# Expert stage of a hybrid decoder step: eight row slots, each waited for on its own, and groups of four experts

## The chip, the cores and the metric

The kernel runs on one core of a Trainium2 chip. The time is the device time of one launch in microseconds (us). Before the change it was 5759.28 us, the median of three runs (5758.3 to 5764.06).

## What is computed

One layer of a decoder: modulated norm, one wide projection, two token mixers, a merge with an output projection, and then an expert layer. Prompt: 1024 tokens of width 1024. Sample group: 8 tokens. The change touches the expert layer alone. For each token it has 8 heads, for each head 16 expert numbers `e` and 16 gates `g` (found earlier), out of 16384 experts. An expert is a row `u` and a row `v` of 1024 float32 numbers each.

```
def one_block(args):
    hb, eb, gb = args
    a = jax.nn.gelu(jnp.einsum('td,thkd->thk', hb, u[eb], preferred_element_type=jnp.float32))
    return jnp.einsum('thk,thkd->td', (gb * a).astype(v.dtype), v[eb])
...
y = rms_norm(x + g2 * peer_ffn(h2, ...), final_g)
```

## The kernel before

The program is a row of stages with a barrier between them: modulation and projection, the prompt's mixers, the sample's mixers, merge and routing, and then `experts`, which starts at about 3025 us and runs to the end. In DRAM the `u` and `v` of an expert stand side by side in one row of 8 KB (`peer_uv`).

The prompt is 8 tiles of 128 tokens, one token on each partition. A tile has 8 heads (`PH`), a head 16 experts (`TOPK`, here `NSLOT`). I call the gather of one expert number for the 128 tokens of a tile a *row load*: one indirect DMA on the GpSimd queue (POOL), 128 rows of 8 KB, 1 MB, into one of the slots `UV[n]` (128 partitions x 2048 numbers). There are 8 x 8 x 16 = 1024 row loads. Each goes through the same steps:

- POOL (L1542 to L1547) waits until the slot is free, which TensorE's semaphore `vdone` tells, and issues the load. Slot `n` holds expert `n` of the head; the waits stand at every fourth expert (`GRP`), and each wants four slots free.
- DVE (L1671 to L1687) waits for a group of four loads (`loaded[n // GRP]`), and multiplies each `u` half with the token's row `h2` and sums it, a *dot* (L1677). After every eighth dot (`SUB`) it works out the weights of those eight: three small steps of the gelu (L1447 to L1449), a tanh on ScalarE (ACT, L1612), two more small steps (L1684, L1687).
- ACT makes from each weight column a diagonal matrix 128 x 128 (L1617).
- TensorE (PE, L1586 to L1592) multiplies the diagonal with the `v` half into a PSUM accumulator, 2 products of 512 columns for each expert, which stand in the trace as four records. Behind the last of them it raises `vdone`, and the slot is free.

The accumulators are `ex_acc` for even tiles, `ex_bc` for odd ones. After the first head of a tile the DVE and ACT programs do the end of the tile before it (`tail`): gate, residual, final norm, store. The order of each engine is written out by hand; nothing is scheduled by a planner.

Ahead of the prompt the stage works the sample's 8 tokens: 8 loads (L1534) into slots 8 to 15 (`HALF + n`), dots, and products (L1572). While it does so, `vdone` already allows the prompt's first eight loads into slots 0 to 7 (`HALF`, L1557); the other eight come free when the sample's last product is done (L1576, L1577).

Of the kernel before, what the change touches and what calls it, by code (L numbers as in the profile page):

```python
# [14 lines left out]
P = 128  # L15
D = 1024
# [3 lines left out]
NS = 8  # L20
# [12 lines left out]
PH, NK, DQ, TOPK = 8, 128, 128, 16  # L33
# [17 lines left out]
def at_least(eng, sem, value):  # L51

    if not isinstance(value, int) or value > 0:
        eng.wait_ge(sem, value)
# [1397 lines left out]
def experts(k, misc):  # L1452

    nc = k.nc
    NSLOT = TOPK
    GRP = 4
    NQ = NSLOT // GRP
    HALF = NSLOT - NS
    names = ("in", "mod", "idxT_ps", "idxT", "bc", "bc_used", "dots", "s_u", "s_exp", "steps", "wm", "s_sum", "s_t", "x1", "sq", "var", "root", "y", "h2_l", "x1_l",
             "staged", "dotted", "g_steps", "g_u", "g_exp", "w", "diag", "vdone", "zero", "tail_t", "t_steps", "y_out", "h2s", "nsel", "tiles_done")  # L1460
    s = {n: k.sem("ex_" + n) for n in names}
    rows_s = [k.sem(f"ex_rows_sample{n}") for n in range(NS)]
    loaded = [k.sem(f"ex_rows_loaded{q}") for q in range(NQ)]
    uv_dram = k.i["peer_uv"]
    SUB = NSLOT // 2
    with k.phase() as f:
        UV = [f.sb(f"ex_UV{n}", [P, 2 * D]) for n in range(NSLOT)]
# [6 lines left out]
        idx = [f.sb(f"ex_idx{b}", [P, NSLOT], U32) for b in range(2)]  # L1474
# [21 lines left out]
        with nc.Block() as block:  # L1496
# [32 lines left out]
            @block.gpsimd  # L1529
            def _(pool):  # L1530

                pool.wait_ge(s["idxT"], 1)
                for n in range(NS):
                    pool.indirect_dma_start(out=UV[HALF + n][:, :], out_offset=None, in_=uv_dram, in_offset=bass.IndirectOffsetOnAxis(ap=idxT[:, n:n + 1], axis=0)).then_inc(rows_s[n], 16)  # L1534


                def head(i, pair, b):

                    h = pair * 2 + b
                    nc.gpsimd.tensor_copy(idx[b][:, :], k.idx[:, bass.ds(i * P + h * NSLOT, NSLOT)]).then_inc(p["staged"], 1)  # L1540
                    pool.wait_ge(p["staged"], i * PH + h + 1)
                    for n in range(NSLOT):  # L1542
                        if n % GRP == 0:
                            pool.wait_ge(p["vdone"], (i * PH + h) * NSLOT + n + GRP)
                            pool.sem_inc(p["zero"], 1)
                        pool.indirect_dma_start(out=UV[n][:, :], out_offset=None, in_=uv_dram,  # L1546
                                                in_offset=bass.IndirectOffsetOnAxis(ap=idx[b][:, n:n + 1], axis=0)).then_inc(loaded[n // GRP], 16)  # L1547

                with pool.Fori(0, TILES) as i:
                    with pool.Fori(0, PH // 2) as pair:  # L1550
                        for b in range(2):
                            head(i, pair, b)

            @block.tensor
            def _(pe):

                pe.sem_inc(p["vdone"], HALF)  # L1557
                nc.tensor.transpose(tp[:, 0:NS], k.idx_s[:, :], ident[SL, SL])
                nc.tensor.transpose(tp[:, NS:2 * NS], k.gate_s[:, :], ident[SL, SL]).then_inc(s["idxT_ps"], 1)
                pe.wait_ge(s["h2s"], 16)  # L1560
                pe.wait_ge(s["nsel"], 1)
                for n in range(NS):
                    at_least(pe, s["dots"], n - 1)
                    for b in range(2):
# [12 lines left out]
                pe.sem_inc(p["vdone"], NSLOT - HALF)  # L1577
                pe.wait_ge(s["tiles_done"], 2)

                def tile(i, j, t):  # L1580
                    acc = accs[t]
                    pe.wait_ge(p["acc_t"], i if not isinstance(i, int) else 1)
                    for b in range(2):
                        nc.tensor.matmul(acc[:, b, :], zb[:, :], zr[:, :], start=True, stop=False)
                    with pe.Fori(0, PH) as h:
                        for n in range(NSLOT):  # L1586
                            if n % GRP == 0:
                                pe.wait_ge(loaded[n // GRP], (i * PH + h) * (16 * GRP) + 16 * GRP)
                            pe.wait_ge(p["diag"], (i * PH + h) * NSLOT + n + 1)
                            for b in range(2):  # L1590
                                last = nc.tensor.matmul(acc[:, b, :], dg[:, n, :], V[n][:, b * 512:(b + 1) * 512], start=False, stop=False)  # L1591
                            last.then_inc(p["vdone"], 1)  # L1592
                    for b in range(2):
                        last = nc.tensor.matmul(acc[:, b, :], zb[:, :], zr[:, :], start=False, stop=True)
                    last.then_inc(p["summed"], 1)
                pairs_of_tiles(pe, tile)

            @block.scalar
            def _(act):
# [7 lines left out]


                def head(i, h):
                    for c in range(2):  # L1610
                        act.wait_ge(p["g_u"], (i * PH + h) * 2 + c + 1)
                        nc.scalar.activation(uu[:, c * SUB:(c + 1) * SUB], uu[:, c * SUB:(c + 1) * SUB], ACT.Tanh, scale=GELU_C).then_inc(p["g_exp"], 1)  # L1612
                        act.wait_ge(p["w"], (i * PH + h) * 2 + c + 1)
                        for n in range(c * SUB, (c + 1) * SUB):

                            act.wait_ge(p["vdone"], (i * PH + h) * NSLOT + n + 1)
                            nc.scalar.activation(dg[:, n, :], ident, ACT.Copy, scale=w[:, n:n + 1]).then_inc(p["diag"], 1)  # L1617

                def tail(i):
# [18 lines left out]
            def _(dve):  # L1638
# [3 lines left out]
                link = chained(dve, s["steps"])  # L1642
# [26 lines left out]
                dve.sem_inc(p["acc_t"], 1)  # L1669

                def head(i, h, hb):  # L1671
                    for c in range(2):
# [8 lines left out]
                        link = chained(dve, p["g_steps"], (i * PH + h) * 6 + c * 3)  # L1681
                        gelu_steps(nc, link, a[:, cols], t[:, cols], uu[:, cols]).then_inc(p["g_u"], 1)
                        dve.wait_ge(p["g_exp"], (i * PH + h) * 2 + c + 1)
                        link(nc.vector.scalar_tensor_tensor(out=t[:, cols], in0=uu[:, cols], scalar=1.0, in1=a[:, cols], op0=ALU.add, op1=ALU.mult))  # L1684
                        gate = k.gate[:, bass.ds(i * P + h * NSLOT + c * SUB, SUB)]
                        at_least(dve, p["diag"], (i * PH + h) * NSLOT + c * SUB - SUB)
# [90 lines left out]
```

## Time and profile before

| | us |
|---|---|
| median of the runs | 5759.28 |
| the profiled execution, its own time | 5768.66 |
| span of its trace | 5766.5 |
| busy in the span: PE | 4560.9 (79%) |
| busy: DVE | 2323.8 (40%) |
| busy: POOL | 1169.3 (20%) |
| busy: ACT | 886.2 (15%) |
| row loads, 1024, POOL | 1083.11 MB on queue q0 |

The profiled execution took 9.4 us longer than the median. Busy shares of the whole span mix stages of quite different kinds, so the stage of the experts is read by itself: first its DMA share and the rate of its transfers, then the times at which single groups land and single slots come free.

### The profile page before, as it was taken

The page shows a single profiled execution, that of the slowest core. Times are in us where ns is not written, and L with a number is a line of the kernel's source. Part 1 is how long each engine was busy: PE and PEld are TensorE (multiplying, and loading weights), DVE is VectorE, ACT ScalarE, POOL GpSimd, SP SyncE. Part 2 cuts the span into 40 slices and gives each one's busy share as a digit, 9 for nine tenths or more (in the row PEclk, how much of TensorE's full clock was granted, in tenths as well). Part 3 has the DMA queues.
Part 4 walks back from the last instruction along what each step waited for, and adds up shares of the span by engine and source line. Part 5 has one row for each costly group of instructions (what it writes and reads, how often), then busy time and mean ns, then how long its engine had stood idle before and what let it go on. Part 6 is the DMA issues. An engine that isn't in the chain of part 4 may idle for free. (4 is left out here: it accounts for less than half of the span.)

```text
span 5766.5 us, 41916 instructions
## 1 busy us (share of the span) xinstructions
PE 4560.9 (79%) x13011; PEld 2177.4 (38%) x13044; DVE 2323.8 (40%) x5481; ACT 886.2 (15%) x1951; POOL 1169.3 (20%) x1104
## 2 busy tenths in 40 slices
PE   6999999977777767888837777777777777777777
PEld 1444444434544543344312333333333333333333
DVE  2000000003333334388894554454544445454544
ACT  1100000012222220121101111111111111111111
POOL 0000000000000000000004444444444444444443
PEclk8999999987777776899977888888888898889888
DMA  7143444462101023311009999999999999999997
GB/s 260 53 156 136 149 156 156 166 208 92 42 35 57 31 76 136 140 47 47 28 3 367 411 409 412 405 402 400 407 401 401 407 408 412 408 411 410 410 405 313
DMA packets 247745, 1409.28 MB, mean 244 GB/s; under 512 B 24467, under 2 KB 76179, under 8 KB 110804
## 3 DMA queue, kind: packets, MB, share of 16 engines
q0 software_dynamic: 148896, 1083.11, 46.0%
q1 hardware_dynamic: 72118, 272.53, 13.4%
q10 hardware_dynamic: 26672, 52.88, 2.4%
q8 instruction: 33, 0.54, 0.0%
q14 instruction: 26, 0.21, 0.0%
HBM read 1341.66 MB, written 159.08 MB: 260 GB/s over the span
## 5 line engine op out<-in xcount | busy, mean ns | idle before, releaser
L1677 DVE CUSTOM_DVE_ANT_0 ex_UV<-ex_UV,ex_h 128x1024 f32<-128x1024 f32 x1024 | 1194.0, 1221 | 1211.9 <-DMA ex_UV<-in_peer_uv,ex_idx 1211.9
L1546 POOL DMA_INDIRECT ex_UV<-in_peer_uv,ex_idx x1024 | 1135.0, 1108 | 1534.5 <-PE ex_acc L1591 630.5
L1591 PE MATMUL ex_acc<-ex_UV,ex_diag 128*128 128x512 f32 x2048 | 1015.8, 659 | 320.2 <-ACT ex_diag L1617 320.2
L1591 PE MATMUL ex_bc<-ex_UV,ex_diag 128*128 128x512 f32 x2048 | 1008.9, 656 | 318.1 <-ACT ex_diag L1617 318.1
L406 PE MATMUL z_ps<-win,hT 128*128 128x464 f32 x2688 | 1055.2, 554 | 22.3 <-ACT z_stage L383 11.6
L1591 PEld LDWEIGHTS ex_acc<-ex_UV,ex_diag 128*128 128x128 f32 x2048 | 429.3, 213 | 905.8 <-issue 526.6
L1591 PEld LDWEIGHTS ex_bc<-ex_UV,ex_diag 128*128 128x128 f32 x2048 | 425.9, 211 | 899.7 <-issue 519.6
L406 PEld LDWEIGHTS z_ps<-win,hT 128*128 128x128 f32 x2688 | 510.9, 191 | 555.9 <-issue 537.4
L763 DVE TENSOR_SCALAR mx_gn<-mx_gn 128x1024 f32<-128x1024 f32 x1 | 0.7, 694 | 1136.8 <-DMA mx_gn<-in_gla_gn_g 1136.8
L1534 POOL DMA_INDIRECT ex_UV<-in_peer_uv,ex_idxT x8 | 7.6, 953 | 1740.9 <-DVE ex_idxT L1646 1738.8
L1612 ACT ACTIVATE ex_u<-ex_u 128x8 f32<-128x8 f32 x128 | 26.7, 209 | 2130.0 <-DVE ex_u L1449 2130.0
L1617 ACT ACTIVATE ex_diag<-misc,ex_w 128x128 f32<-128x128 f32 x1024 | 312.9, 388 | 88.8 <-DVE ex_w L1687 88.8
L488 POOL DMA_DIRECT2D mx_masks<-table_masks x1 | 0.7, 706 | 1274.8 <-POOLq L150 1274.8
L383 ACT COPY z_stage<-z_ps 128x464 f32<-128x464 f32 x168 | 91.6, 546 | 991.5 <-PE z_ps L406 961.5
L1218 PE MATMUL rt_G<-rt_wO,rt_Tg 128*128 128x512 f32 (+1 forms) x288 | 146.7, 674 | 9.2 <-ACT rt_Tg L1270 9.2
L819 DVE TENSOR_REDUCE mx_max<-mx_big 128x1 f32<-128x1920 f32 x32 | 69.0, 2158 | 162.4 <-PE mx_big L622 162.4
L1218 PE MATMUL rt_G<-rt_wQ,rt_Tg 128*128 128x512 f32 (+1 forms) x288 | 127.2, 600 | 9.1 <-ACT rt_Tg L1270 9.1
L1218 PE MATMUL rt_G<-rt_wA,rt_Tm 128*128 128x512 f32 (+1 forms) x288 | 128.1, 604 | 7.8 <-DMA rt_wA<-in_w_branch_a 7.8
L636 PE MATMUL mx_T<-misc,mx_P 128*128 128x128 f32 x480 | 68.0, 285 | 66.3 <-DVE mx_PT L832 55.9
L615 PE MATMUL mx_big<-mx_kT,mx_qT 128*128 128x512 f32 x128 | 88.8, 784 | 28.0 <-DVE mx_kT L761 26.4
L1218 PEld LDWEIGHTS rt_G<-rt_wO,rt_Tg 128*128 128x128 f32 (+1 forms) x288 | 58.2, 206 | 92.5 <-issue 81.0
L653 PE MATMUL mx_O<-mx_V,mx_PT 128*128 128x128 f32 (+1 forms) x480 | 79.9, 343 | 11.2 <-DVE mx_PT L832 6.7
(332 smaller groups left out, 3399.5 us busy)
## 6 DMA issues: line engine op xcount, KB each, us to landing
out_kv_w_sample<-in_cache_kv_w SPq DMA_DIRECT2D x8, 8188.0 KB, 42.7
win<-in_w_in SPq DMA_DIRECT2D x21, 1856.0 KB, 11.4
z_scratch<-z_stage ACTq DMA_DIRECT2D x21, 1856.0 KB
ada<-in_ada_w SPq DMA_DIRECT2D x12, 2048.0 KB, 7.8
ex_UV<-in_peer_uv,ex_idx POOLq DMA_INDIRECT x1024, 8.5
out_kv_w_sample<-in_cache_kv_w SPq DMA_DIRECT2D x8, 2044.0 KB, 18.1
mx_zg<-z_scratch SPq DMA_DIRECT2D x8, 1544.0 KB, 7.1
mx_zq<-z_scratch SPq DMA_DIRECT2D x8, 1536.0 KB, 10.1
```

The source lines that it names most:

```text
L383: nc.scalar.copy(zst[u][:, t, :], pz[t % NBK][:, 0:W]).then_inc(evac, 1)
L406: last = nc.tensor.matmul(pz[t % NBK][:, 0:W], hT[:, c, t * P:t * P + P], w[u][:, c, :], start=(c == 0), stop=(c == KD - 1))
L615: nc.tensor.matmul(big[:, b, :], qT[:, 8 + h, :], kT[:, 8 + h, b * 512:(b + 1) * 512], start=False, stop=True)
L636: last = nc.tensor.transpose(Tb[b % 2][:, (j % 4) * P:(j % 4 + 1) * P], Pm[:, j * P:(j + 1) * P], ident)
L653: last = nc.tensor.matmul(OM[h % 2][:, 0:HD], PT[h % 2][:, j, :], vv, start=(j == 0), stop=(j == KT - 1))
L819: nc.vector.reduce_max(mx[:, h:h + 1], sc_all[:, 0:NKEY], AX.X).then_inc(s["max_steps"], 1)
L1218: last = nc.tensor.matmul(G[0:R, bank + b, :], T[:, off + c, 0:R], w[:, c, b * 512:(b + 1) * 512], start=(c == 0), stop=(c == n - 1))
L1546: pool.indirect_dma_start(out=UV[n][:, :], out_offset=None, in_=uv_dram, in_offset=bass.IndirectOffsetOnAxis(ap=idx[b][:, n:n + 1], axis=0 ...
L1591: last = nc.tensor.matmul(acc[:, b, :], dg[:, n, :], V[n][:, b * 512:(b + 1) * 512], start=False, stop=False)
L1612: nc.scalar.activation(uu[:, c * SUB:(c + 1) * SUB], uu[:, c * SUB:(c + 1) * SUB], ACT.Tanh, scale=GELU_C).then_inc(p["g_exp"], 1)
L1617: nc.scalar.activation(dg[:, n, :], ident, ACT.Copy, scale=w[:, n:n + 1]).then_inc(p["diag"], 1)
L1677: nc.vector.tensor_tensor_reduce(out=U[n], in0=U[n], in1=hb, scale=1.0, scalar=0.0, op0=ALU.mult, op1=ALU.add, accum_out=a[:, n:n + 1]).th ...
```

## The change

There are eight slots in place of sixteen. Expert `n` of a head goes into slot `n % 8`. Each slot has a semaphore of its own, and DVE, PE and POOL wait for each single slot where they waited for four. The weights of a head are worked out in four groups of four experts (`SUB = 4`) where there were two of eight. The sample's 8 loads now take all eight slots (`HALF = 8 - 8 = 0`), so that the line that allowed eight of the prompt's loads ahead of the sample's end falls away.

```
-    GRP = 4
-    NQ = NSLOT // GRP
-    HALF = NSLOT - NS
+    NBUF = 8
+    ROUNDS = NSLOT // NBUF
+    HALF = NBUF - NS
...
-    SUB = NSLOT // 2
+    SUB = 4
+    SUBS = NSLOT // SUB
...
                     for n in range(NSLOT):
-                        if n % GRP == 0:
-                            pool.wait_ge(p["vdone"], (i * PH + h) * NSLOT + n + GRP)
-                            pool.sem_inc(p["zero"], 1)
-                        pool.indirect_dma_start(out=UV[n][:, :], out_offset=None, in_=uv_dram,
-                                                in_offset=bass.IndirectOffsetOnAxis(ap=idx[b][:, n:n + 1], axis=0)).then_inc(loaded[n // GRP], 16)
+                        pool.wait_ge(p["vdone"], (i * PH + h) * NSLOT + n + 1)
+                        pool.sem_inc(p["zero"], 1)
+                        pool.indirect_dma_start(out=UV[n % NBUF][:, :], out_offset=None, in_=uv_dram,
+                                                in_offset=bass.IndirectOffsetOnAxis(ap=idx[b][:, n:n + 1], axis=0)).then_inc(loaded[n % NBUF], 16)
...
-                pe.sem_inc(p["vdone"], HALF)
...
                 pe.wait_ge(s["s_sum"], 1)
-                pe.sem_inc(p["vdone"], NSLOT - HALF)
+                pe.sem_inc(p["vdone"], NBUF - HALF)
...
-                            if n % GRP == 0:
-                                pe.wait_ge(loaded[n // GRP], (i * PH + h) * (16 * GRP) + 16 * GRP)
+                            pe.wait_ge(loaded[n % NBUF], ((i * PH + h) * ROUNDS + n // NBUF) * 16 + 16)
...
-                    for c in range(2):
+                    for c in range(SUBS):
...
-                            act.wait_ge(p["vdone"], (i * PH + h) * NSLOT + n + 1)
+                            at_least(act, p["vdone"], (i * PH + h) * NSLOT + n + 1 - (NSLOT - NBUF))
...
-                            if n % GRP == 0:
-                                dve.wait_ge(loaded[n // GRP], (i * PH + h) * (16 * GRP) + 16 * GRP)
-                            nc.vector.tensor_tensor_reduce(out=U[n], in0=U[n], in1=hb, scale=1.0, scalar=0.0, op0=ALU.mult, op1=ALU.add,
+                            dve.wait_ge(loaded[n % NBUF], ((i * PH + h) * ROUNDS + n // NBUF) * 16 + 16)
+                            nc.vector.tensor_tensor_reduce(out=U[n % NBUF], in0=U[n % NBUF], in1=hb, scale=1.0, scalar=0.0, op0=ALU.mult, op1=ALU.add,
```

How this stands on the engines, at the two places that matter. First POOL, the first loads of a prompt head, before (`ex_UV4` is slot 4, `ep_vdone` the semaphore of the free slots):

```order
L1546 DMA ex_UV0<-in_peer_uv,ex_idx0 128x2048 [waits ep_vdone]
L1546 DMA ex_UV1<-in_peer_uv,ex_idx0 128x2048
L1546 DMA ex_UV2<-in_peer_uv,ex_idx0 128x2048
L1546 DMA ex_UV3<-in_peer_uv,ex_idx0 128x2048
L1544 REGISTER_ALU
L1546 DMA ex_UV4<-in_peer_uv,ex_idx0 128x2048 [waits ep_vdone]
```

And in the changed kernel:

```order
L1546 DMA ex_UV0<-in_peer_uv,ex_idx0 128x2048 [waits ep_vdone]
L1544 REGISTER_ALU
L1546 DMA ex_UV1<-in_peer_uv,ex_idx0 128x2048 [waits ep_vdone]
L1544 REGISTER_ALU
L1546 DMA ex_UV2<-in_peer_uv,ex_idx0 128x2048 [waits ep_vdone]
L1544 REGISTER_ALU
L1546 DMA ex_UV3<-in_peer_uv,ex_idx0 128x2048 [waits ep_vdone]
```

A load can now be issued as soon as its one slot is free, where it waited for the fourth of its group; the ninth load of a head goes into slot 0 again, where it had slot 8.

Second DVE, in a tile's first head, around the first weights. Before (each dot is an `ISA` row with a second one that reads the sum; semaphores have kept the names of an earlier stage, `mx_T_free0` is here the one of loads 8 to 11):

```order
L1677 ISA ex_UV6,ex_a<-ex_UV6,ex_h20 128x1024
L1677 ISA ex_a 128x1
L1677 ISA ex_UV7,ex_a<-ex_UV7,ex_h20 128x1024
L1677 ISA ex_a 128x1
L1447 TENSOR_TENSOR ex_t<-ex_a 128x8 [waits sm_state_loaded3]
L1448 TENSOR_SCALAR ex_t<-ex_t 128x8 [waits sm_state_loaded4]
L1449 TENSOR_TENSOR ex_u<-ex_t,ex_a 128x8 [waits sm_state_loaded4]
L1684 SCALAR_TENSOR_TENSOR ex_t<-ex_u,ex_a 128x8 [waits sm_state_loaded6]
L1687 SCALAR_TENSOR_TENSOR ex_w<-ex_t,expert_gate 128x8 [waits sm_state_loaded4]
L1677 ISA ex_UV8,ex_a<-ex_UV8,ex_h20 128x1024 [waits mx_T_free0]
```

And in the changed kernel (`mx_T_free1` is the semaphore of slot 3, `sm_state_loaded1` that of slot 4):

```order
L1674 ISA ex_UV3,ex_a<-ex_UV3,ex_h20 128x1024 [waits mx_T_free1]
L1674 ISA ex_a 128x1
L1447 TENSOR_TENSOR ex_t<-ex_a 128x4 [waits sm_state_loaded7]
L1448 TENSOR_SCALAR ex_t<-ex_t 128x4 [waits ep_g_steps]
L1449 TENSOR_TENSOR ex_u<-ex_t,ex_a 128x4 [waits ep_g_steps]
L1681 SCALAR_TENSOR_TENSOR ex_t<-ex_u,ex_a 128x4 [waits ep_g_exp]
L1684 SCALAR_TENSOR_TENSOR ex_w<-ex_t,expert_gate 128x4 [waits ep_g_steps]
L1674 ISA ex_UV4,ex_a<-ex_UV4,ex_h20 128x1024 [waits sm_state_loaded1]
```

The weights follow the fourth dot, where they followed the eighth, and every dot has a wait of its own.

## Rows read from the trace of the kernel before

**Rows 1.** Windows: busy time by engine, two stretches of the prompt's experts.
```profile
core 0: us, PE busy (x) PEld busy (x) DVE busy (x) ACT busy (x) POOL busy (x), PEclk, DMA share, GB/s
3440.00:4440.00 1000.00, 763.06 (x1528) 322.07 (x1530) 500.12 (x1022) 162.14 (x465) 423.81 (x404) 0.87 0.99 405
4440.00:5440.00 1000.00, 757.34 (x1555) 320.28 (x1558) 501.05 (x1025) 162.19 (x465) 431.96 (x410) 0.88 1.00 409
```

**Rows 2.** Timeline of DVE in one head: start, length, first dots of groups.
```profile
4165.11 1.23 DVE L1677 CUSTOM_DVE_ANT_0 ex_UV<-ex_UV,ex_h 128x1024 f32<-128x1024 f32 x1 [6.11 <-DMA ex_UV<-in_peer_uv,ex_idx]
...
4175.05 1.22 DVE L1677 CUSTOM_DVE_ANT_0 ex_UV<-ex_UV,ex_h 128x1024 f32<-128x1024 f32 x1 [5.27 <-DMA ex_UV<-in_peer_uv,ex_idx]
...
4178.49 1.22 DVE L1677 CUSTOM_DVE_ANT_0 ex_UV<-ex_UV,ex_h 128x1024 f32<-128x1024 f32 x1
...
4184.99 1.22 DVE L1677 CUSTOM_DVE_ANT_0 ex_UV<-ex_UV,ex_h 128x1024 f32<-128x1024 f32 x1 [3.63 <-DMA ex_UV<-in_peer_uv,ex_idx]
```

**Rows 3.** Timeline of POOL in the same head: issues of row loads.
```profile
4150.99 0.96 POOL L1546 DMA_INDIRECT ex_UV<-in_peer_uv,ex_idx  x1 [12.34 <-PE ex_bc L1591]
...
4155.17 1.99 POOL L1546 DMA_INDIRECT ex_UV<-in_peer_uv,ex_idx  x1 [0.30 <-issue]
...
4192.35 0.96 POOL L1546 DMA_INDIRECT ex_UV<-in_peer_uv,ex_idx  x1 [10.28 <-PE ex_bc L1591]
```

**Rows 4.** Windows of 5 us in the same head, columns as in rows 1.
```profile
4140.00:4145.00 5.00, 4.84 (x6) 2.19 (x7) 2.10 (x3) 2.15 (x8) 0.00 (x0) 0.50 1.01 423
...
4150.00:4155.00 5.00, 5.00 (x13) 2.28 (x12) 2.17 (x3) 0.00 (x0) 3.27 (x3) 1.00 0.58 195
```

**Rows 5.** The line of the row loads, L1546: summary, and issue to landing.
```profile
L1546 POOL DMA_INDIRECT ex_UV<-in_peer_uv,ex_idx x1016: 932/938/10366, 3080.0 to 5719.1; - x170
...
DMA to landing us min/median/max: 5.4/8.4/12.1
```

**Rows 6.** Timeline of PE: three bursts of eight experts, 32 records each.
```profile
4140.16 16.87 PE L1591 MATMUL ex_bc<-ex_UV,ex_diag 128*128 128x512 f32 x32 [9.29 <-ACT ex_diag L1617]
4159.57 15.70 PE L1591 MATMUL ex_bc<-ex_UV,ex_diag 128*128 128x512 f32 x32 [2.54 <-ACT ex_diag L1617]
4181.93 16.47 PE L1591 MATMUL ex_bc<-ex_UV,ex_diag 128*128 128x512 f32 x32 [6.66 <-ACT ex_diag L1617]
```

**Rows 7.** Chain that ended last: start, length; PE for four experts, then POOL.
```profile
3115.61 7.15 PE ex_acc L1591 x16
...
4159.57 8.84 PE ex_bc L1591 x16
...
4169.21 1.37 POOL ex_UV L1546
```

**Rows 8.** DMA issues: KB each, us to landing.
```profile
ex_h<-h_scratch SPq DMA_DIRECT2D x8, 512.0 KB, 12.4
ex_x<-x_scratch SPq DMA_DIRECT2D x8, 512.0 KB, 8.2
out_y_prompt<-ex_y ACTq DMA_DIRECT2D x8, 512.0 KB, 9.2
```

**Rows 9.** Timeline of POOL at the start of the prompt's experts.
```profile
3046.16 0.93 POOL L1546 DMA_INDIRECT ex_UV<-in_peer_uv,ex_idx  x1 [0.30 <-issue]
3079.96 0.94 POOL L1546 DMA_INDIRECT ex_UV<-in_peer_uv,ex_idx  x1 [32.86 <-PEq L1577]
```

**Rows 10.** Timeline of DVE at a tile's end: last dot, last weights, first dot behind the tail.
```profile
3774.39 1.22 DVE L1677 CUSTOM_DVE_ANT_0 ex_UV<-ex_UV,ex_h 128x1024 f32<-128x1024 f32 x1
...
3776.94 0.17 DVE L1687 SCALAR_TENSOR_TENSOR ex_w<-ex_t,expert_gate 128x8 f32<-128x8 f32 x1
...
3783.65 1.22 DVE L1677 CUSTOM_DVE_ANT_0 ex_UV<-ex_UV,ex_h 128x1024 f32<-128x1024 f32 x1
```

**Rows 11.** Timeline of DVE at the end of the kernel.
```profile
5755.40 1.23 DVE L1696 TENSOR_TENSOR ex_y<-ex_bc,ex_g 128x1024 f32<-128x1024 f32 x1 [16.73 <-PE ex_bc L1594]
```

More of the change, by code:

```diff
@@ L1462, in experts @@
     rows_s = [k.sem(f"ex_rows_sample{n}") for n in range(NS)]
-    loaded = [k.sem(f"ex_rows_loaded{q}") for q in range(NQ)]
+    loaded = [k.sem(f"ex_slot_loaded{n}") for n in range(NBUF)]
     uv_dram = k.i["peer_uv"]
-    SUB = NSLOT // 2
+    SUB = 4
+    SUBS = NSLOT // SUB
     with k.phase() as f:
-        UV = [f.sb(f"ex_UV{n}", [P, 2 * D]) for n in range(NSLOT)]
+        UV = [f.sb(f"ex_UV{n}", [P, 2 * D]) for n in range(NBUF)]
         U = [t[:, 0:D] for t in UV]
@@ L1586, in tile @@
                         for n in range(NSLOT):
-                            if n % GRP == 0:
-                                pe.wait_ge(loaded[n // GRP], (i * PH + h) * (16 * GRP) + 16 * GRP)
+                            pe.wait_ge(loaded[n % NBUF], ((i * PH + h) * ROUNDS + n // NBUF) * 16 + 16)
                             pe.wait_ge(p["diag"], (i * PH + h) * NSLOT + n + 1)
                             for b in range(2):
-                                last = nc.tensor.matmul(acc[:, b, :], dg[:, n, :], V[n][:, b * 512:(b + 1) * 512], start=False, stop=False)
+                                last = nc.tensor.matmul(acc[:, b, :], dg[:, n, :], V[n % NBUF][:, b * 512:(b + 1) * 512], start=False, stop=False)
                             last.then_inc(p["vdone"], 1)
@@ L1609, in head @@
                 def head(i, h):
-                    for c in range(2):
-                        act.wait_ge(p["g_u"], (i * PH + h) * 2 + c + 1)
+                    for c in range(SUBS):
+                        act.wait_ge(p["g_u"], (i * PH + h) * SUBS + c + 1)
                         nc.scalar.activation(uu[:, c * SUB:(c + 1) * SUB], uu[:, c * SUB:(c + 1) * SUB], ACT.Tanh, scale=GELU_C).then_inc(p["g_exp"], 1)
-                        act.wait_ge(p["w"], (i * PH + h) * 2 + c + 1)
+                        act.wait_ge(p["w"], (i * PH + h) * SUBS + c + 1)
                         for n in range(c * SUB, (c + 1) * SUB):
-                            act.wait_ge(p["vdone"], (i * PH + h) * NSLOT + n + 1)
+                            at_least(act, p["vdone"], (i * PH + h) * NSLOT + n + 1 - (NSLOT - NBUF))
                             nc.scalar.activation(dg[:, n, :], ident, ACT.Copy, scale=w[:, n:n + 1]).then_inc(p["diag"], 1)
@@ L1671, in head @@
                 def head(i, h, hb):
-                    for c in range(2):
+                    for c in range(SUBS):
                         cols = slice(c * SUB, (c + 1) * SUB)
                         for n in range(c * SUB, (c + 1) * SUB):
-                            if n % GRP == 0:
-                                dve.wait_ge(loaded[n // GRP], (i * PH + h) * (16 * GRP) + 16 * GRP)
-                            nc.vector.tensor_tensor_reduce(out=U[n], in0=U[n], in1=hb, scale=1.0, scalar=0.0, op0=ALU.mult, op1=ALU.add,
+                            dve.wait_ge(loaded[n % NBUF], ((i * PH + h) * ROUNDS + n // NBUF) * 16 + 16)
+                            nc.vector.tensor_tensor_reduce(out=U[n % NBUF], in0=U[n % NBUF], in1=hb, scale=1.0, scalar=0.0, op0=ALU.mult, op1=ALU.add,
                                                            accum_out=a[:, n:n + 1]).then_inc(p["dotted"], 1)
@@ L1680, in head @@
                         dve.sem_inc(p["dots_done"], SUB)
-                        link = chained(dve, p["g_steps"], (i * PH + h) * 6 + c * 3)
+                        link = chained(dve, p["g_steps"], ((i * PH + h) * SUBS + c) * 3)
                         gelu_steps(nc, link, a[:, cols], t[:, cols], uu[:, cols]).then_inc(p["g_u"], 1)
-                        dve.wait_ge(p["g_exp"], (i * PH + h) * 2 + c + 1)
+                        dve.wait_ge(p["g_exp"], (i * PH + h) * SUBS + c + 1)
                         link(nc.vector.scalar_tensor_tensor(out=t[:, cols], in0=uu[:, cols], scalar=1.0, in1=a[:, cols], op0=ALU.add, op1=ALU.mult))
                         gate = k.gate[:, bass.ds(i * P + h * NSLOT + c * SUB, SUB)]
-                        at_least(dve, p["diag"], (i * PH + h) * NSLOT + c * SUB - SUB)
+                        at_least(dve, p["diag"], (i * PH + h) * NSLOT + c * SUB + SUB - NSLOT)
                         nc.vector.scalar_tensor_tensor(out=w[:, cols], in0=t[:, cols], scalar=0.5, in1=gate, op0=ALU.mult, op1=ALU.mult).then_inc(p["w"], 1)
```

## The prediction, made before the changed kernel ran

> **What bounds the kernel now.** I read the windows first, then the timelines of DVE, POOL and PE in one head. In the windows the prompt's experts run at a DMA share of 0.99 to 1.00 and 405 to 409 GB/s, while PE, DVE and POOL have idle time [rows 1]. So the row loads set the pace. The timeline of DVE gives the pace exactly: groups of four loads that follow each other on a full queue are 9.94 us apart (4165.11, 4175.05, 4184.99) [rows 2], 2.485 us for a load, 39.76 us for a head of sixteen. The loads of the whole stage are slower than that. From the first issue after the sample's part (3080.0) to the last (5719.1) there are 1016 of them [rows 5], 2639.1 / 1015 = 2.600 us each, 41.60 us a head. Some of the difference is other traffic: three transfers of 512 KB per tile [rows 8], which at the loads' own rate (1024 KB in 2.485 us) are 3.7 us a tile, 0.45 us a head. The rest, 41.60 - 39.76 - 0.45 = 1.4 us a head, is a queue that runs dry. The reader sees it in the window from 4150 to 4155, where the share is 0.58 and the rate 195 GB/s [rows 4]: the load issued at 4150.99 [rows 3] found next to nothing ahead of it.
>
> Why it runs dry is a loop, which I take apart because the change shortens the loop and its allowance together. The slot of expert 0 is loaded from 4150.99 and loaded again from 4192.35 [rows 3], 41.36 us later. In between: 14.12 us until the four loads of the group have landed and DVE starts on them (4165.11) [rows 2, 3]; 9.94 until the second group is there (4175.05); 3.44 until DVE is at the last of its four dots (4178.49) [rows 2]; 3.44 for this dot, the gelu steps, tanh, weights and the first diagonal, until PE starts (4181.93) [rows 6]; and 10.42 for PE's first four experts and the way back to POOL [rows 3, 6]. The allowance for this loop is a full queue with sixteen slots, 39.76 us. The loop is longer, so it sets the pace of a head, and DMA waits for it. That is the step on which everything below rests: **the time for which a slot is away from the queue**, against the time that the other slots' loads last.
>
> **The loop of the change.** The allowance falls to eight loads, 8 x 2.485 = 19.88 us. What a slot needs from issue to issue, for the first expert of a group of four, which waits longest:
> - Until the fourth load of its group has landed and DVE starts on its dot: 14.12 us as above [rows 2, 3]. The other three dots are done by then, since they no longer wait for the group; the 3.44 us of dots are gone. This is the value for a queue that was almost empty at issue. Bounds: a load alone on the queue takes 5.4 us [rows 5] and three more 7.46, together 12.9; with more ahead of it the time is longer, but then DMA is not waiting.
> - From the start of the last dot to PE's start: 3.44 us, unchanged; the small steps are on 4 columns in place of 8, and their length is their start-up.
> - PE on the first expert. Four experts took 7.15 us at the full clock and 8.84 us with a slow start [rows 7]. One expert at the full clock is a quarter of 7.15, so 1.8; all of the slow start lies in the first, so it is 1.8 + 1.7 = 3.5. Here the clock matters: PE's granted clock is 0.50 of full, the lower level of 1.2 GHz, in the 5 us in which a burst starts after 9.29 us of idle, and 1.00 later in that burst [rows 4, 6]; a burst after 2.54 us of idle still took 15.70 us and one after 6.66 us 16.47 [rows 6], where 32 records at the full rate would be about 14. In the changed kernel PE works 7 to 9 us of every 10 and idles 2 to 3, near the first of these. I take 2.9 for the first expert, a little above the middle.
> - From PE's end to POOL's issue: 0.80 us (8.84 us from 4159.57, issue at 4169.21) [rows 7].
>
> Sum: 14.12 + 3.44 + 2.9 + 0.8 = **21.3 us against an allowance of 19.9**. Two groups pass per loop, so a head takes 42.6 us, and with the other traffic 43.05, against 41.60. The second to fourth experts wait less for their group (by 2.485 each) and only a fully slow start of PE brings them level. The halved number of slots is thus paid for mostly, but not wholly, by what is taken out of the loop: 41.36 goes to 21.3 and not to 20.7, and even that would leave no gain.
>
> **The other parts, each once.**
> - *Start.* Eight of the prompt's loads were issued during the sample's part, the last at 3046.16, and the ninth at 3079.96 [rows 9]. Now the first can go only at 3079.96, as all eight slots hold the sample's rows. That is eight loads more behind this point, 8 x 2.600 = +20.8 us. Nothing covers it, since DMA is what the stage waits for.
> - *Tails.* After a tile's first head DVE is away for 6.5 us (3777.11 to 3783.65). From the start of the last dot (3774.39) to the end of the tail it is 9.3 us [rows 10]; then four dots, 1.15 us apart, are waiting, and the last starts at 12.7 where it could at 10.65. Of the sixteen slots, eight were loaded and covered it. Now it stretches one loop in seven tiles by 2 us: +14.
> - *End.* Before, from the time at which a 1025th load would have been issued (3080.0 + 1016 x 2.600 = 5721.6) to the end there are 44.9 us. After, the last group of four is issued 10.65 before that point, lands 14.12 later, PE starts 3.44 later and does four experts in 8.84 instead of eight in 15.70 [rows 6, 7]; then as now 11.1 us from DVE's L1696 (5755.40) to the end [rows 11], and 0.5 between. That is 27.3 us: -17.6.
> - *More instructions.* 128 more rounds of five small DVE steps and one tanh, and waits for each slot on DVE, PE, POOL. DVE is busy half of the stage [rows 1]; a round is done 2.7 us after the start of the last dot (3774.39 to 3777.11) [rows 10], of which 1.2 are the dot, and the next load lands 2.5 to 3 us after that start. Nothing. If the cover went, it would be 128 x 1.5, 190 us.
> - *ACT's wait* for `vdone` asks for the same expert of the head before, as it did, and costs nothing.
>
> Sum: 64 heads x (43.05 - 41.60) = +92.8; +20.8; +14; -17.6; together **+110 us**. Against the span of 5766.5 that is 5876; the profiled execution lay 9.4 us above the median, so against the median of 5759.3 it is **5870 us**.
>
> How sharp this is: a head takes twice the loop, so 1 us in the loop is 128 us in the time. No change in the total would need a loop of 20.4 us.
>
> **A rule against it.** The rows give a load by itself 5.4 us from issue to landing at the least [rows 5]. The Trainium skill, "DMA: Bandwidth & Descriptors", section on the anatomy of one DMA on the GpSimd path, puts a fixed 2.0 us on each such DMA and moves the bytes at 436 GB/s, by which 1 MB takes an estimated 4.4 us. With that in place of the row the loop would be 20.3, and the time 5742, slightly faster than before. I go by the row.
>
> **The rivals.**
> - *The queue stays full (faster).* All loads land at the lone load's 5.4 us and the 2.485 of its followers, 12.9 us, since they are now issued one by one and not four at a time, and PE starts its short bursts mostly at the full clock, 1.8 us. Loop 12.9 + 3.44 + 1.8 + 0.8 = 18.9, under the allowance. A head is then 39.76 + 0.45 = 40.2: 64 x -1.4 = -90, with +20.8, +14, -17.6 it is -73: 5686 us. In between, loops from 20.0 to 20.3 give 5705 to 5745. For it: PE idles least in this scheme; the shares in the windows were already near 1. Against it: after 2.54 us of idle PE still started slowly [rows 6], and the measured group took 14.12. It decides below a loop of 20.4. Chance 0.14.
> - *It cancels out.* A loop of 20.4 to 20.6 leaves the time within 12 us of before. Chance 0.07.
> - *POOL is held up as well (much slower).* An issue that stands beside a dot took 1.99 us where others take 0.96 [rows 3]. The dots now spread over half of the time, at one every 2.5 us, and each single issue is on the loop. With 1.0 us more for this, and a slow first expert each time (3.5), the loop is 22.9, a head 46.2: +294 and +17, 6070 us. Against it: the average issue beside dots is only a few tenths longer (431.96 us for 410 instructions in 1000 us [rows 1]). The Trainium skill, "SBUF — State Buffer", section "Who interferes with whom", says that a DVE instruction with two SBUF inputs holds up a GpSimd one that reads SBUF, until it is done; the 1.99 us agree with that. Chance of anything above 5970: 0.13.
> - *The waits for single slots do nothing*, because DVE is late anyway: then the three dots stay in the loop, 24.7 us, and the time is over 6250 us. DVE idles 3.6 to 6.1 us before each group [rows 2], so no; inside the last 0.13.
>
> **How the numbers follow.** The forecast, a loop of 20.6 to 22.1, is 5780 to 5970, chance 0.66. Range: down to 5740, which takes in the cancelling case and the upper part of the faster one, and up to 5970: about 0.8. About 0.2% (12 us) is what can be told from no change. Faster by more than that 0.14, within it 0.07, slower 0.79.
>
> **What will show it.** Right: a DMA share of 0.95 to 0.97 in the stretches of rows 1 and about 395 GB/s; starts of the fourth dots of groups 10.5 to 10.9 us apart; first issue of a prompt's load still near 3080, and none before; PE bursts of 16 records and 7.2 to 9 us, granted clock 0.85 to 0.95. Wrong: groups 9.94 us apart outside the tiles' ends (queue full), POOL issues mostly at 1.9 us, or a first issue that has moved. The forecast fails most easily by the 14.12 us, which was measured on four loads issued at once.

## The result: 4.5% slower, in the direction of the forecast but past its range

| | us |
|---|---|
| before, median of 4 runs | 5761.42 |
| changed, median of 4 runs | 6024.62 |
| ratio, 95% interval | 1.0452 (1.0434 to 1.047) |
| changed, the profiled execution: its own time, span | 6013.12, 6011.0 |
| forecast, range | 5870, 5740 to 5970 |

The forecast said +110 us and the change cost +263. The profile after, windows of the same two stretches as in [rows 1]:

```profile
core 0: us, PE busy (x) PEld busy (x) DVE busy (x) ACT busy (x) POOL busy (x), PEclk, DMA share, GB/s
3440.00:4440.00 1000.00, 728.67 (x1425) 300.99 (x1426) 519.16 (x1166) 164.37 (x476) 408.19 (x374) 0.86 0.94 376
4440.00:5440.00 1000.00, 722.34 (x1417) 297.28 (x1415) 512.18 (x1154) 161.51 (x467) 408.32 (x374) 0.87 0.93 372
```

The DMA share has fallen from 0.99 to 0.94 and the rate from 405 to 376 GB/s, lower than the 395 that the forecast would have needed. The line of the row loads, answering to [rows 5]:

```profile
L1546 POOL DMA_INDIRECT ex_UV<-in_peer_uv,ex_idx x1024: 932/937/2342, 3082.1 to 5978.9; - x171
...
DMA to landing us min/median/max: 5.4/9.4/15.9
```

1023 issue intervals in 2896.8 us are 2.832 us for a load, 45.3 us for a head, where [rows 5] gave 41.6. This accounts for the difference of the spans (6011.0 - 5766.5 = 244.5): 64 heads x 3.71 = +237, eight loads more behind the sample's part and a start 2.1 us later (3082.1 for 3080.0) = +23, and from the last issue to the end 32.1 in place of 47.4 = -15. The sum is 245. The medians differ by 263 because the profiled execution before lay 7.2 us above its median and the one after 11.5 us below.

The loop of a slot in one head, first POOL (answering to [rows 3]; these are the issues of a group's first load), then DVE (the fourth dots), then PE (to [rows 6]):

```profile
4142.98 1.48 POOL L1546 DMA_INDIRECT ex_UV<-in_peer_uv,ex_idx  x1 [8.23 <-PE ex_acc L1589]
...
4165.74 1.60 POOL L1546 DMA_INDIRECT ex_UV<-in_peer_uv,ex_idx  x1 [8.20 <-PE ex_acc L1589]
...
4187.86 0.94 POOL L1546 DMA_INDIRECT ex_UV<-in_peer_uv,ex_idx  x1 [7.42 <-PE ex_bc L1589]
```

```profile
4157.80 1.22 DVE L1674 CUSTOM_DVE_ANT_0 ex_UV<-ex_UV,ex_h 128x1024 f32<-128x1024 f32 x1 [1.27 <-DMA ex_UV<-in_peer_uv,ex_idx]
...
4167.73 1.23 DVE L1674 CUSTOM_DVE_ANT_0 ex_UV<-ex_UV,ex_h 128x1024 f32<-128x1024 f32 x1 [1.22 <-DMA ex_UV<-in_peer_uv,ex_idx]
...
4179.66 1.22 DVE L1674 CUSTOM_DVE_ANT_0 ex_UV<-ex_UV,ex_h 128x1024 f32<-128x1024 f32 x1 [1.26 <-DMA ex_UV<-in_peer_uv,ex_idx]
```

```profile
4161.14 9.06 PE L1589 MATMUL ex_acc<-ex_UV,ex_diag 128*128 128x512 f32 x16 [5.69 <-ACT ex_diag L1615]
4171.00 7.13 PE L1589 MATMUL ex_acc<-ex_UV,ex_diag 128*128 128x512 f32 x16 [0.80 <-ACT ex_diag L1615]
...
4183.27 6.93 PE L1589 MATMUL ex_bc<-ex_UV,ex_diag 128*128 128x512 f32 x9 [4.27 <-ACT ex_diag L1615]
```

Two loops are 22.76 and 22.12 us, where I forecast 21.3. And the two groups of a loop are not alike: fourth dots stand 9.93 us apart (4157.80, 4167.73) and then 11.93 (4179.66). One group rides close behind the other at the full queue's pace, and the whole gap stands before the first. So PE has one long idle time per loop, 5.69 us here, and not two of 2 to 3. Averaged over the heads (five and later), it idles 5.0 us before the first group of a head and the third, and 1.3 before the other two. The burst after the long idle takes 9.06 us, with a granted clock of 0.50 from 4161.14 to 4165; the one after 0.80 us takes 7.13. The chain of waits shows what the slow start costs on the loop, answering to [rows 7]:

```profile
4161.14 3.80 PE ex_acc L1589 x4
4164.98 0.55 issue
...
4165.74 1.09 POOL ex_UV L1546
```

The first expert takes 3.80 us, and 0.80 more pass until POOL issues. Single loops differ: in the second one above the landing took 13.92 us (4165.74 to 4179.66), less than the 14.12 of the forecast, and the rest was longer. So the terms are compared as averages below.

### The profile page after: what moved, and what is told of

Read it like the earlier page. It is cut to its first block and busy times, and to the rows that moved or that the text cites. A ratio compares the mean times of both kernels' runs of the same rounds, so it can differ in the third digit from the quotient of the medians.

```text
span 6011.0 us, 45440 instructions
## 1 busy us (share of the span) xinstructions
PE 4644.1 (77%) x13044; PEld 2190.6 (36%) x13044; DVE 2484.7 (41%) x6121; ACT 926.1 (15%) x2079; POOL 1206.1 (20%) x1104
## 3 DMA queue, kind: packets, MB, share of 16 engines
q1 hardware_dynamic: 72118, 272.53, 12.9%
## 5 line engine op out<-in xcount | busy, mean ns | idle before, releaser
L1674 DVE CUSTOM_DVE_ANT_0 ex_UV<-ex_UV,ex_h 128x1024 f32<-128x1024 f32 x1024 | 1254.0, 1226 | 1210.4 <-DMA ex_UV<-in_peer_uv,ex_idx 1195.1
L1546 POOL DMA_INDIRECT ex_UV<-in_peer_uv,ex_idx x1024 | 1164.5, 1137 | 1755.3 <-PE ex_acc L1589 769.5
L1589 PE MATMUL ex_acc<-ex_UV,ex_diag 128*128 128x512 f32 x2048 | 1049.2, 672 | 405.7 <-ACT ex_diag L1615 405.5
L1589 PE MATMUL ex_bc<-ex_UV,ex_diag 128*128 128x512 f32 x2048 | 1052.5, 674 | 398.0 <-ACT ex_diag L1615 397.5
L1610 ACT ACTIVATE ex_u<-ex_u 128x4 f32<-128x4 f32 x256 | 52.6, 206 | 2243.8 <-DVE ex_u L1449 2243.8
L1615 ACT ACTIVATE ex_diag<-misc,ex_w 128x128 f32<-128x128 f32 x1024 | 327.2, 390 | 176.3 <-DVE ex_w L1684 171.0
## 6 DMA issues: line engine op xcount, KB each, us to landing
win<-in_w_in SPq DMA_DIRECT2D x21, 1856.0 KB, 11.5
out_kv_w_sample<-in_cache_kv_w SPq DMA_DIRECT2D x8, 2044.0 KB, 18.3
```

Source lines behind the costliest of these rows:

```text
L1546: pool.indirect_dma_start(out=UV[n % NBUF][:, :], out_offset=None, in_=uv_dram, in_offset=bass.IndirectOffsetOnAxis(ap=idx[b][:, n:n + 1], ...
L1589: last = nc.tensor.matmul(acc[:, b, :], dg[:, n, :], V[n % NBUF][:, b * 512:(b + 1) * 512], start=False, stop=False)
L1674: nc.vector.tensor_tensor_reduce(out=U[n % NBUF], in0=U[n % NBUF], in1=hb, scale=1.0, scalar=0.0, op0=ALU.mult, op1=ALU.add, accum_out=a[: ...
```

## What the experiments tell apart

My theory after the result: time = 64 heads x 2 loops. A loop is made of four terms, the landing (first issue of a group to its fourth dot), the way from the dot to PE, PE's first expert, and the way back to POOL, and only what exceeds the time of the other slots' loads counts. Rivals: the small steps and waits that were added are the cost; eight slots are too few whatever the loop; the slow start of PE is covered; POOL's issues are held up by the dots.

To compare kernels by these terms I averaged them over the groups of a head five and later, from the issues of POOL, the dots of DVE and PE's records in the timelines (first expert here: from the start of its first record to the start of the next expert's). A and B are the two groups of a loop, slots 0 to 3 and 4 to 7; in most loops the long idle time of PE stands before A.

| kernel | landing A / B | dot to PE | first expert A / B | to POOL | loop | allowed |
|---|---|---|---|---|---|---|
| changed | 15.0 / 16.3 | 3.4 | 3.3 / 2.0 | 1.0 | 22.7 | 20.1 |
| dots by four | 18.3 / 20.0 | 3.3 | 3.5 / 1.8 | 1.0 | 26.2 | 20.1 |
| POOL by four | 14.2 / 16.3 | 3.3 | 3.6 / 1.8 | 6.3 | 27.5 | 20.1 |
| products of zeros | 15.5 / 15.6 | 3.4 | 2.0 / 1.9 | 1.0 | 21.9 | 20.1 |
| h2 in PSUM | 15.0 / 15.9 | 3.4 | 3.1 / 2.2 | 1.0 | 22.4 | 20.1 |
| both | 15.3 / 15.4 | 3.4 | 2.0 / 1.8 | 1.0 | 21.7 | 20.1 |
| one product | 15.5 / 15.6 | 3.3 | 1.8 / 1.8 | 1.0 | 21.7 | 20.1 |
| groups of two | 14.0 / 14.0 | 3.4 | 1.9 / 1.8 | 1.0 | 20.3 | 20.1 |
| sixteen slots | 33.6 / 34.0 | 3.4 | 2.4 / 2.1 | 1.0 | 40.4 | 40.2 |

"Allowed" is 19.88 or 39.76 us of loads with 0.22 or 0.45 for the other transfers. In the last two the landing is mostly time in a full queue.

### Sixteen slots again, all else of the change

```
-    NBUF = 8
+    NBUF = 16
...
+                pe.sem_inc(p["vdone"], HALF)
```

> Sixteen slots again, and the eight loads ahead of the sample's end, with all else of the change: a wait for each single slot and four groups of four experts. Theory (the loop of a slot, issue to issue, against the time that the other slots' loads last): the loop is about 22.4 us as measured in the changed kernel, the allowance 39.76 us, so the queue never runs dry: 39.76 + 0.45 for other transfers = 40.2 us a head, 1.4 less than before, 64 x 1.4 = 90 us, and the end about 10 shorter: about 5670 us. Rival (the single waits and the doubled rounds of small steps are what costs, not the slots): near 6000 us, or at least not under 5760.

Measured: 5683.4 us, ratio to before 0.986 (0.9843 to 0.9878), 13 us above what the theory gave and far from the rival. The windows, same columns as above, have a full queue:

```profile
3440.00:4440.00 1000.00, 771.58 (x1593) 317.75 (x1592) 577.60 (x1304) 185.66 (x533) 459.42 (x420) 0.93 1.01 422
```

The waits for single slots and the doubled rounds of small steps are all in this kernel, so they are not what costs. The same waits and groups on eight slots take 6024.6 us, on sixteen 5683.4 (some 20 us of this are the eight loads ahead, below).

### Eight slots, groups of two

```
-    SUB = 4
+    SUB = 2
```

> The changed kernel with eight slots, but weights in eight groups of two experts. Theory (a slot waits for its group): the first expert waits for one load in place of three, the loop is 22.4 - 2 x 2.485 = 17.4 us, under the allowance of 19.88, and the queue stays full: 40.2 us a head, and with the later start (+21) and the end (-20) about 5680 us. Rival (eight slots are too few whatever the group): about 6020 us. Second rival (DVE's rounds of small steps, 1.5 us for every two dots, delay dots and landings): between 5750 and 6000.

Measured: 5700.7 us, ratio 0.9898 (0.9881 to 0.9915). So eight slots are enough when the loop is short enough: two loads less to wait for, 5 us, and the loop is at its allowance. The time is 20 us above the theory, as a head took 40.5 us and not 40.2.

```profile
3440.00:4440.00 1000.00, 735.64 (x1579) 287.14 (x1578) 647.43 (x1785) 214.68 (x626) 501.28 (x416) 0.98 1.01 418
```

The first rival (too few whatever the group) falls, and the second as well, though DVE is busy 65% of the time now. The loop is the cause, not the count.

### DVE, and then POOL, by four again

```
-                            dve.wait_ge(loaded[n % NBUF], ((i * PH + h) * ROUNDS + n // NBUF) * 16 + 16)
+                            if n % 4 == 0:
+                                for m in range(n, n + 4):
+                                    dve.wait_ge(loaded[m % NBUF], ((i * PH + h) * ROUNDS + m // NBUF) * 16 + 16)
```

> The changed kernel, but DVE waits for all four loads of a group before the first dot, as the kernel before did; POOL still goes slot by slot. Theory: three dots, 3.44 us, come back into the loop, 22.4 to 25.9; a head becomes 6.9 us longer, 64 x 6.9 = 440: about 6465 us. Rival (the waits on single slots bring nothing): 6020 us.

Measured: 6459.4 us (two runs). The loop is 26.2, 3.5 more, the three dots.

```
-                        pool.wait_ge(p["vdone"], (i * PH + h) * NSLOT + n + 1)
-                        pool.sem_inc(p["zero"], 1)
+                        if n % 4 == 0:
+                            pool.wait_ge(p["vdone"], (i * PH + h) * NSLOT + n + 4)
+                            pool.sem_inc(p["zero"], 1)
```

> The changed kernel, but POOL waits for four free slots before it issues four loads, as the kernel before did; DVE still goes slot by slot. Theory: loop = 14.1 to landing + 3.4 + TensorE's four experts 9 with a slow start + 1.0 = 27.5, a head 55.5 with other traffic: 64 x (55.5 - 45.3) = 650 more: about 6670 us. Rival (single waits at POOL bring nothing): 6020 us.

Measured: 6629.8 us (two runs), 40 below the expectation; the loop is 27.5 as expected, but a head is 55.0 and not 55.5. Here four loads are issued together on an empty queue. POOL's first issues of two groups stand 27.53 us apart, and DVE's fourth dot of the first of them, the last row here, 14.43 us after its first issue:

```profile
4154.17 0.94 POOL L1547 DMA_INDIRECT ex_UV<-in_peer_uv,ex_idx  x1 [13.82 <-PE ex_acc L1590]
...
4181.70 0.96 POOL L1547 DMA_INDIRECT ex_UV<-in_peer_uv,ex_idx  x1 [14.29 <-PE ex_acc L1590]
```

```profile
4168.60 1.22 DVE L1675 CUSTOM_DVE_ANT_0 ex_UV<-ex_UV,ex_h 128x1024 f32<-128x1024 f32 x1 [1.25 <-DMA ex_UV<-in_peer_uv,ex_idx]
```

The averages in the table give 14.2 for such a group, which is the 14.12 of the forecast. So each of the two waits, taken by itself, is worth what the sum of the loop says: 3.5 us of loop at DVE (435 us), 4.8 at POOL (605 us). What the change took out of the loop was real.

### Keep PE busy

```
+        idle = f.ps("ex_idle", [P, 512])
...
                             last.then_inc(p["vdone"], 1)
+                            if n % SUB == SUB - 1:
+                                for _ in range(12):
+                                    nc.tensor.matmul(idle[:, :], zb[:, :], zr[:, :], start=True, stop=True)
```

> The changed kernel, and behind every fourth expert TensorE does 12 products of zeros (bfloat16, 512 columns, about 2.6 us) into an unused PSUM bank, so that it idles little. They are added work and change no result. Theory (each loop has a slow start of TensorE in it, because the two groups of a loop run together and it then idles 4 to 6 us): the first expert of every group takes 1.8 in place of 3.6 us, the loop falls from 22.4 to 20.6, and a head by 3.6 us: 64 x 3.6 = 230 less than the changed kernel, about 5790 us, with a granted clock near 1.00. Rival (the slow start is covered, the loads' landing and POOL set the loop): 6020 us, or more by the added products.

Measured: 5915.1 us, ratio 1.0265 (1.0248 to 1.0282): 110 us less than the changed kernel, though PE has more to do. The slow start is thus on the path. But it is half of what I expected. PE's rows, and the windows:

```profile
4151.75 7.13 PE L1590 MATMUL ex_bc<-ex_UV,ex_diag 128*128 128x512 f32 x16 [0.85 <-ACT ex_diag L1619]
4158.72 2.75 PE L1594 MATMUL ex_idle<-ex_zero_row,ex_zero 128*128 128x512 bf16 x12
4161.93 7.13 PE L1590 MATMUL ex_bc<-ex_UV,ex_diag 128*128 128x512 f32 x16 [0.46 <-ACT ex_diag L1619]
```

```profile
3440.00:4440.00 1000.00, 907.25 (x2571) 385.79 (x2569) 536.77 (x1203) 169.98 (x492) 424.76 (x387) 0.98 0.98 389
```

Nearly every burst takes 7.0 to 7.2 us and the granted clock is 0.98. The first expert gave back its 1.3 us in group A, but the landing grew from 15.0 to 15.5, so the loop fell by 0.8 and not by 1.8. Where the landing goes is seen between two groups. DVE's dots for the last load of one group and the first two of the next, and POOL's issue of that first one:

```profile
4158.59 1.23 DVE L1678 CUSTOM_DVE_ANT_0 ex_UV<-ex_UV,ex_h 128x1024 f32<-128x1024 f32 x1 [1.25 <-DMA ex_UV<-in_peer_uv,ex_idx]
4162.63 1.22 DVE L1678 CUSTOM_DVE_ANT_0 ex_UV<-ex_UV,ex_h 128x1024 f32<-128x1024 f32 x1 [1.26 <-DMA ex_UV<-in_peer_uv,ex_idx]
4165.12 1.23 DVE L1678 CUSTOM_DVE_ANT_0 ex_UV<-ex_UV,ex_h 128x1024 f32<-128x1024 f32 x1 [1.26 <-DMA ex_UV<-in_peer_uv,ex_idx]
```

```profile
4154.54 1.01 POOL L1547 DMA_INDIRECT ex_UV<-in_peer_uv,ex_idx  x1 [4.37 <-PE ex_bc L1590]
```

The load was issued 4.05 us before the one ahead of it landed. By a lone load's 5.4 us it could have been there at 4159.9, and behind the other at 4161.1. It came at 4162.6, 8.1 us after its issue, and 4.04 behind the load ahead in place of 2.49. This is one load, and the trace as a whole bears it out: where DVE stood waiting for a load, those issued 4 to 5 us before the landing ahead of them (60 loads) came 3.55 us behind it on average, those issued 5 to 6 us before it (68 loads) 2.59. So a load that reaches a queue in which little is left loses time that neither its own 5.4 us nor its place in the queue explains.

### Is it POOL, held up by the dots?

```
-                    hb = h2s[b][:, :]
+                    hb = bc[1][:, :, :].rearrange("p b n -> p (b n)")
                     dve.wait_ge(h2_l[b], 16 * j + 16)
+                    nc.vector.tensor_copy(hb, h2s[b][:, :]).then_inc(p["h2_ps"], 1)
+                    dve.wait_ge(p["h2_ps"], i + 1)
```

> The changed kernel, but the token rows h2 that the dots read lie in PSUM (the sample's second broadcast buffer, copied there by DVE once per tile, about 1.3 us x 8), so that a dot has one operand in SBUF in place of two. Theory A (a dot holds up the issue that stands beside it, and a held issue lands later): issues of 1.9 us become 0.94, and the 15.0 to 15.6 us from a group's first issue to its fourth dot become about 14.1; the loop falls by 0.9 to 1.4, 64 x 2 of that: 115 to 180 us less than the changed kernel, 5845 to 5910. Theory B (the landing is long because loads come one by one behind the other group's): no change beyond the copies, 6020 to 6035.

Measured: 5992.9 us, ratio 1.0402 (1.0384 to 1.0419). The groups of instructions between 3440 and 5440 us, first of the changed kernel, then of this one (count, busy time, mean ns, idle before):

```profile
L1546 POOL DMA_INDIRECT ex_UV<-in_peer_uv,ex_idx x704 | 800.7, 1137 | 1183.8 <-PE ex_bc L1589 569.6 <-PE ex_acc L1589 483.7 <-issue 126.0
```

```profile
L1546 POOL DMA_INDIRECT ex_UV<-in_peer_uv,ex_idx x715 | 670.8, 938 | 1327.3 <-PE ex_bc L1589 694.2 <-PE ex_acc L1589 607.6 <-issue 25.5
```

The hold-up is gone altogether: the mean issue fell from 1137 to 938 ns, the length of a free one. The time lies between the two theories. Of theory A the first half holds (a dot holds up the issue beside it), the second does not (a held issue lands later): group A's landing stayed at 15.0. The worth of it all, with the cost of the eight copies in it, is 32 us, not 115 to 180.

> Both: h2 in PSUM, and 12 products of zeros behind every fourth expert. Theory A with the slow start: landing 14.1, 3.4, first expert 1.9, back to POOL 1.0: loop 20.4, a head 41.3 with other traffic: about 5770 us. Theory B: as with the products alone, 5915 us.

Both together: 5895.1 us, ratio 1.0227 (1.021 to 1.0244), 125 us above my expectation. The loop is 21.7, with a landing of 15.3 and 15.4 where I had put 14.1. That is 20 us less than with the products alone, so theory B misses as well, by little.

### PE with half the work

```
-                            for b in range(2):
+                            for b in range(1):
                                 last = nc.tensor.matmul(acc[:, b, :], dg[:, n, :], V[n % NBUF][:, b * 512:(b + 1) * 512], start=False, stop=False)
```

> The changed kernel with only the first 512 columns of each expert's product; the other half of the output rows is left without its expert sum, and TensorE's work is halved. Theory 1 (fixed landing): the first expert takes 1.8 in place of 3.4 us, the loop falls from 22.7 to 21.1, 64 x 2 x 1.6 = 205 us less than the changed kernel: 5820. Theory 2 (what TensorE gives is partly taken back, since loads issued earlier find more of the other group ahead of them and the queue's near-dry packets are slow, as the products of zeros suggested): about half of that, 5900 to 5930.

Measured: 5896.9 us (two runs), 3 us below the range of theory 2 and far from theory 1. The first expert takes 1.8 us, with no added products, and the landing is 15.5 again; the loop comes to the same 21.7. So it was not the products of zeros that stood in the way: a faster PE and a PE with half the work end at much the same landing, 15.3 to 15.6.

```profile
3440.00:4440.00 1000.00, 547.19 (x750) 209.69 (x749) 541.36 (x1215) 170.14 (x492) 418.75 (x394) 0.73 0.99 392
```

The DMA share is 0.99 here, but the rate is 392 GB/s; with sixteen slots it was 422 at 1.01. The engines are busy and move less, so part of the loss doesn't show as idle time. The single packets of the trace show where it is. A packet of a row load is one row of 8 KB. Between 3440 and 5440 us it took 314 ns on average with sixteen slots, and 0.02% of the packets took over 400 ns. In the changed kernel it was 327 ns and 4.4%, with one product 330 ns and 5.1%, the longest 2.3 us. The median is 309 to 311 ns in all three. So in a nearly dry queue a few packets take far longer than the rest. The late load in the kernel with the products of zeros shows both this and engines without work: between 4157.5 and 4161, 13.9 packets were in flight on average where it was 16.2 from 4151 to 4154, and the longest took 1.97 us.

### The start, and each part of the change alone on sixteen slots

```
-                pe.sem_inc(p["vdone"], HALF)
...
-                pe.sem_inc(p["vdone"], NBUF - HALF)
+                pe.sem_inc(p["vdone"], NBUF)
```

(against the kernel with sixteen slots above)

> Sixteen slots with single waits and four groups, but none of the prompt's loads may go before the sample's part is over (as in the changed kernel). Against sixteen slots with the eight loads ahead (5683 us) this prices the start alone. Theory: eight loads more behind that point at the full queue's pace, 8 x 2.52 = 20 us: 5703 us. Rival (other waits in the start cover them): 5683 us.

Measured: 5698.1 us, 14.7 more than with the loads ahead. The intervals of the two against before overlap (0.9859 to 0.9895 here, 0.9843 to 0.9878 there), so the traces are the better measure. The first row load of the expert stage, first of this kernel, then of the one with the loads ahead:

```profile
3029.24 1.01 POOL L1535 DMA_INDIRECT ex_UV<-in_peer_uv,ex_idxT  x1 [1738.87 <-DVE ex_idxT L1644]
```

```profile
3039.03 1.01 POOL L1535 DMA_INDIRECT ex_UV<-in_peer_uv,ex_idxT  x1 [1749.56 <-DVE ex_idxT L1645]
```

The stages ahead, which the edit does not touch, took 10 us longer in the second. From these rows to the ends of the spans (5696.8 and 5685.5) it is 2667.6 and 2646.5 us: the start costs 21.1, as the theory has it.

The waits for single slots alone (`SUB = 8` in the kernel with sixteen slots):

> The kernel before with one part of the change alone, the waits for single slots at POOL, DVE and PE: sixteen slots, weights in two groups of eight. Theory: the loop loses DVE's three dots and three of TensorE's experts, 14.1 + 9.9 + 3.4 + 3.6 + 1.0 = 32 us of 39.8, so the queue stays full: 40.4 us a head, 5690 us (the end is up to 8 us longer than with groups of four). Rival (groups of four are needed as well): 5760 us.

Measured: 5675.4 us, ratio 0.9843 (0.9826 to 0.986), 15 below the theory. The groups of four alone, on the kernel before:

```
-    SUB = NSLOT // 2
+    SUB = 4
+    SUBS = NSLOT // SUB
...
```

> The kernel before with the other part alone: weights in four groups of four; sixteen slots, and all waits for four at a time as they were. Theory: the first group no longer waits for the second, loop = 14.1 + 3.4 of dots + 3.4 + 9.0 + 1.0 = 31 us of 39.8, the queue stays full: about 5690 us. Rival: 5760 us.

Measured: 5679.9 us, ratio 0.9853 (0.9835 to 0.987), 10 below the theory. And groups of two with single waits:

> Sixteen slots, waits for each slot, weights in eight groups of two. Theory (the queue is full with four groups already): the same 40.4 us a head as with four groups, and an end shorter by two experts, 3.5 us: about 5680 us, no difference that can be told from sixteen slots with four groups (5683). Rival (a shorter loop still helps): under 5660.

Measured: 5686.2 us, ratio 0.9867 (0.9851 to 0.9884). The four kernels with sixteen slots and the loads ahead lie within 11 us of each other, and their intervals overlap. Either part of the change alone brings the loop under 39.8 us, and the second one brings nothing. All of them beat the changed kernel, and the kernel before by 79 to 92 us; the smallest edit among them is the groups of four alone, the three lines shown and the counters that follow from them.

## Why the forecast was right in direction and wrong in size

- **What bounds the kernel, and the loop as the step on which all rests: right.** Before, 41.36 us of loop against 39.76 allowed. Bringing the loop under the allowance, in four ways, gave a full queue each time. With eight slots, groups of two did the same.
- **What the change takes out of the loop: right.** The three dots (3.44 forecast, 3.5 measured) and three experts at POOL.
- **The loop of the change, 21.3: too short, the step that failed.** It was 22.7 on average, of which about 0.2 is the other transfers that I had counted by the head. At 128 us for each us of loop, the heads cost 237 us in place of 107 (93 and 14 for the tails). Two terms were mis-sized:
  - *PE's first expert, 2.9 and 0.8 to POOL.* I let PE idle twice per loop for 2 to 3 us, and took a value between the two clocks. The groups ran in pairs, PE idled once for about 5 us, and the group behind the idle time has a slow first expert on its way: 3.80 and 0.80 in the chain shown, 3.3 and 1.0 on average. By the averages 0.6 us too small, some 75 us. The 110 us that busy PE gave back are no check of this: there the first expert fell by 1.3 us and the landing rose by 0.5.
  - *The landing, 14.12.* It holds for four loads issued together on an empty queue (14.2 with POOL by four). In the changed kernel it was 15.0 on average, 0.9 more, some 110 us and so the larger part of the miss, and 15.5 once the rest of the loop was shorter. I had named this term as the one most likely to fail, but set its bound below, at 12.9, and for the far side only said that DMA would not be waiting then. That reasoning is wrong: with 4 us of loads ahead, DMA did wait (4.04 us between two landings).
- **Start, +20.8:** alone, 21.1 between the traces. **End, -17.6:** -15.3. Near enough.
- **Tails, +14:** nothing to be seen. Averaged over the tiles, the head after a tail took 48.0 us where the others took 45.0 (issue to issue): 3.0, which the three transfers of 3.7 us cover. Before it was 45.3 for 41.2.
- **More instructions, nothing: right,** as the sixteen-slot kernels show.
- **The rival of a full queue:** its loop of 18.9 asked for a landing of 12.9. With eight slots and groups of four no kernel had an average below 14.2.
- **The rival of POOL held up:** its time (6070) came closest to the result, by luck in one term. Its slow first expert was near (3.5 for 3.3), but the 1.0 us for held issues was not: the hold-up is real and gone with h2 in PSUM, but worth 32 us, a quarter of a us of loop. The Trainium skill, "SBUF — State Buffer", section "Who interferes with whom", says that with at most one operand in SBUF such a DVE instruction does not contend with GpSimd; the mean of 938 ns agrees.
- **The lone load by the Trainium skill** ("DMA: Bandwidth & Descriptors", the anatomy of one DMA), an estimated 4.4 us, would have given a loop of 20.3. No run of this case had a landing that short; the least was 5.4 in the changed kernel and 5.3 with POOL by four.

**What stays open.** Why a load that meets a nearly empty queue lands late. It is neither POOL's hold-up (taken away, 15.0 and 15.3) nor PE (halved, 15.5). The packets show that it happens in both ways, engines without work and single packets of up to 2 us in place of 0.31. Why these packets take so long, the runs don't show.

## What to carry to other kernels

When a buffer's count and its loop are halved together, compare each with the other: count x time of a load against the time from issue to issue. The loop needs a margin below the allowance, since near the edge terms get longer, by a queue that is nearly dry and by an engine that starts slowly behind each gap: a loop that summed to 20.4 us against 20.1 came out at 21.7, one that summed to 17.4 ran at the allowance. What lies between wasn't run, so the size of the margin stays open. And once the queue is full, a shorter loop is worth nothing, so take the smallest edit that fills it: here one part of the change alone, on the slots that were there.

## What the runs showed of the hardware that I had not expected

- Two groups in flight need not spread out evenly. In the changed kernel they close up, 9.93 and 11.93 us apart, and most of the idle time falls before one of them, where PE then starts at the lower clock (granted 0.50): 9.06 us for 16 records behind 5.69 us of idle, 7.13 behind 0.80.
- 12 added products behind each group, work for nothing, made the kernel 110 us faster, with the granted clock at 0.98 in place of 0.86 and the first expert at 2.0 us in place of 3.3.
- A row load issued 4.05 us ahead of the landing before it came 4.04 us behind that one, and not 2.49; it holds on average too, 3.55 us behind for loads issued 4 to 5 us ahead and 2.59 for those issued 5 to 6 us ahead. The rate at nearly the same DMA share was 7% lower with a nearly dry queue (392 GB/s at 0.99, 422 at 1.01), as 5.1% of the 8 KB packets took over 400 ns where 0.02% did with sixteen slots.
- A dot with one operand in PSUM doesn't hold up the issues beside it: 938 ns on average for 1137.
